# ScalarE's order of two steps in the expert loop of a hybrid transformer trunk

## The reference

```python
def swiglu(x, wg, wu, wd):
    return (jax.nn.silu(x @ wg) * (x @ wu)) @ wd

def moe_ffn(x, router_w, wg, wu, wd):          # D_FF_EXPERT = 1408, N_EXPERTS = 8, TOP_K = 2
    logits = (x @ router_w).astype(jnp.float32)
    top_val, top_idx = lax.top_k(logits, TOP_K)
    w = jax.nn.softmax(top_val, axis=-1)
    gate = jnp.sum(jax.nn.one_hot(top_idx, N_EXPERTS, dtype=jnp.float32) * w[..., None], axis=-2).astype(x.dtype)
    y = jnp.zeros_like(x)
    for e in range(N_EXPERTS):
        y = y + gate[..., e:e + 1] * swiglu(x, wg[e], wu[e], wd[e])
    return y
```

## Time and profile before

| | us |
|---|---|
| median of three timed runs | 1394.48 |
| lowest and highest of them | 1392.77, 1395.32 |
| the profiled execution | 1394.32 |
| its span, first to last instruction | 1392.5 |
| mean granted TensorE clock in it | 0.991 of full speed |

### The profile page before, as it was taken

How to read it: one execution, slowest core, us unless ns; L and a number is a source line. 1 busy time by engine, 2 the same in 40 slices (tenths; PEclk the granted TensorE clock), 3 DMA queues, 4 the chain that set the end, 5 groups by cost and what they waited for, 6 DMA issues and landing times.

```text
span 1392.5 us, 25141 instructions
## 1 busy us (share of the span) xinstructions
PE 1318.3 (95%) x10385; PEld 818.8 (59%) x10385; DVE 995.9 (72%) x1611; ACT 680.9 (49%) x1018; POOL 131.5 (9%) x113
## 2 busy tenths in 40 slices
PE   7999899999999999999999899989999999999992
PEld 4357444444444444444356444569979988978971
DVE  6986797685640456334986886678788888888886
ACT  6245675353210232112245764365576676676672
POOL 0010420410000000030001000501200000000003
PEclk9999999999999999999999999999999999999996
DMA  9330784334220343015220000158999999999975
GB/s 320 106 91 16 257 294 136 136 136 167 106 91 0 136 170 132 0 31 212 71 84 24 16 1 16 61 200 334 360 375 360 322 337 378 357 330 367 343 272 198
DMA packets 39999, 255.70 MB, mean 184 GB/s; under 512 B 5626, under 2 KB 6650, under 8 KB 25418
## 3 DMA queue, kind: packets, MB, share of 16 engines
q1 hardware_dynamic: 30490, 220.20, 42.7%
q0 software_dynamic: 8960, 33.26, 7.2%
q10 hardware_dynamic: 432, 0.59, 0.1%
HBM read 218.28 MB, written 33.65 MB: 181 GB/s over the span
## 4 chain that ended last, share of the span: by engine, by line
PE 75%; DVE 14%; ACT 6%; issue 2%; DMA 2%; SPq 0%; POOL 0%; ACTq 0%; DVEq 0%
PE bank L1117 19%; PE bank L1119 18%; PE bank L1118 18%; DVE arena L928 6%; ACT arena L785 5%; PE bank L1338 3%; PE bank L1384 2%; PE bank L1354 2%; DVE bank L2108 2%; DVE arena L2131 2%; PE bank L1245 1%; PE bank L1182 1%; PE bank L1244 1%; PE bank L1232 1%; ACT arena L1654 1%
## 5 line engine op out<-in xcount | busy, mean ns | idle before, releaser
L928 DVE SCALAR_TENSOR_TENSOR arena<-arena 128x3072 f16<-128x3072 f32 x86 | 288.8, 3358 | 57.1 <-ACT arena L785 56.4
L785 ACT ACTIVATE arena<-arena 128x3072 f16<-128x3072 f32 x86 | 237.0, 2756 | 0.1
L1117 PE MATMUL bank<-arena 128*128 128x144 bf16 (+3 forms) x894 | 219.4, 264 | 11.5 <-DVE arena L928 5.1
L1119 PE MATMUL bank<-arena 128*128 128x144 bf16 (+3 forms) x894 | 219.2, 264 | 0.0
L1118 PE MATMUL bank<-arena 128*128 128x144 f16 (+3 forms) x894 | 219.2, 264 | 0.0
L1117 PE MATMUL bank<-hh,wring_hi 128*128 128x512 bf16 x352 | 133.9, 381 | 0.0
L1119 PE MATMUL bank<-hh,wring_lo 128*128 128x512 bf16 x352 | 133.7, 380 | 0.0
L1118 PE MATMUL bank<-hl,wring_hi 128*128 128x512 f16 x352 | 133.7, 380 | 0.0
L1119 PE MATMUL bank<-hh,arena 128*128 128x512 bf16 x338 | 128.1, 379 | 0.0
L1118 PE MATMUL bank<-hl,arena 128*128 128x512 f16 x338 | 128.1, 379 | 0.0
L1117 PE MATMUL bank<-hh,arena 128*128 128x512 bf16 x338 | 128.1, 379 | 0.0
(11 more groups left out here) (336 smaller groups left out, 2669.8 us busy)
## 6 DMA issues: line engine op xcount, KB each, us to landing
arena<-in_ew SPq DMA_DIRECT2D x86, 1536.0 KB, 9.0
arena<-in_dw SPq DMA_DIRECT2D x22, 1536.0 KB, 6.7
wstage<-in_w_chunk SPq DMA_DIRECT2D x44, 512.0 KB, 3.6
expert_results<-iota POOLq DMA_DIRECT2D x9, 2048.0 KB
arena<-in_cmp_w SPq DMA_DIRECT2D x2, 2048.0 KB, 9.8
expert_slots<-iota POOLq DMA_DIRECT2D x5, 512.0 KB
expert_results<-wstage SPq DMA_DIRECT2D x5, 512.0 KB
arena<-in_w_tok SPq DMA_DIRECT2D x2, 1096.0 KB, 7.1
```

What stands on the lines that cost most here:

```text
L785: act.activation(ew_hi_[:, G % EP, :], ew[:, G % ES, :], ACT.Copy, scale=SW).then_inc(M["hi_ready"], 1)
L928: dve.scalar_tensor_tensor(out=ew_lo_[:, G % EP, :], in0=ew[:, G % ES, :], scalar=SW, in1=ew_hi_[:, G % EP, :], op0=ALU.mult, op1=ALU.subt ...
L1117: pe.matmul(out, w_hi, x_hi, start=first, stop=False)
L1119: return pe.matmul(out, w_lo, x_hi, start=False, stop=last)
```

## The change

ScalarE's order within a chunk is turned round from chunk 11 on (the second expert, n = 1). There `expert_hi(G + 2)` stands ahead of the wait for `up_mm` and the SiLU of chunk G. In chunks 0 to 10 the order stays. Its own waits (DMA of chunk G + 2, `down_stream(G - 2)`), its size and count stay as they are, and nothing is changed on any other engine.

```diff
@@ -65,6 +65,7 @@
 LEAD = 2
+FIRST_TURN = FE // P
 NEG = -1.0e30
@@ -842,11 +843,13 @@
                 first_hi(p)
             for G in range(NG):
                 n, f = divmod(G, FC)
+                if FIRST_TURN <= G < NG - LEAD:
+                    expert_hi(act, G + LEAD)
                 act.wait_ge(M["up_mm"], G + 1)
                 if G >= 2:
                     act.wait_ge(M["product"], FC + G - 1)
                 silu(G % 2, bank[G % 2], CAPS[n])
-                if G < NG - LEAD:
+                if G < FIRST_TURN:
                     expert_hi(act, G + LEAD)
                 if G == LEAD:
                     act.wait_ge(*ready("lg_sub"))
```

## The result

The changed kernel takes **1377.3 us** (median of 4 runs, 1375.79 to 1378.96) against 1393.91 us for the kernel before (4 runs, 1392.77 to 1395.32): 16.6 us less, a ratio of 0.9878 with a 95% interval of 0.9866 to 0.9890. In a second comparison it was 1376.8 against 1392.87, ratio 0.9883 (0.9868 to 0.9899).

What follows compares the result with a forecast made beforehand. The bound was a ring of matmuls, SiLU, upper half and lower half. TensorE's 17.5 us of idle time, less 2, 1, 1.2, 0.8 and 2.5 us, left a 10 us gain: 1384.3 us, range 1379.5 to 1393.

Steps and rivals of the forecast that it cites:

- the ring: Matmuls, SiLU, upper half, lower half, matmuls wait for each other in turn: 9.27 us per two chunks in expert 7.
- the place of the gain: TensorE's waits for VectorE's lower halves in the expert loop, to fall from 12.5 to 5 us or less.
- expert 2 unchanged: Expert 2 (width 168), where TensorE's busy time already fills the length, should keep its 56.8 us.
- the shape of the new waits: VectorE's waits for upper halves under 15 us, from 47.4; ScalarE waits for TensorE's down ahead of the upper half.
- the transfers' rate is no floor: Against a rival, 13%: about 357 GB/s is the average to be had in the experts, giving about 1392 us.
- The ceiling: All TensorE idle time in the waits for lower halves: 12.5 us in 31 waits plus 0.16 each, 17.5 us.
- The start of each expert: Previous expert's results wait for a down at f = 0; 0.7 us stays at experts 3, 5 and 7, 2 us.
- Waits that stay: First two waits of expert 1 (chunks 12 and 13), 1 us; steps to wide experts 2 and 4, 1.2 us.
- VectorE is the fullest: Last five chunks of expert 7: VectorE needs 4.14 us a chunk against TensorE's 3.99, costing 0.8 us.
- The loads: Weight loads landing in 9.8 us make upper halves wait, 4.28 us a chunk; with a border loss, 2.5 us.
- L + 7.3: Loop of four chunks: landing time L, then upper half 2.76, SiLU to product 0.3, product 0.8, lower half 3.4 us.
- the rate in experts 1 and 3: Sign of the forecast: the DMA rate in experts 1 and 3 should rise to 375 GB/s or more.

Runs made afterwards that it cites:

- short loads: Changed kernel, loading only the gate and up parts of each chunk (1024 of 1536 KB) from chunk 22 on: 1376.96 us.
- one chunk less of lead: Kernel before and changed kernel, each load issued one chunk later from chunk 22 on: 1413.08 us in the old order, 1421.94 in the changed order.
- the same kernel: Changed kernel with the turned order from chunk 0 on instead of chunk 11: 1381.9 us in its first run, 1382.18 in its second.
- the kernel turned only in the narrow experts: Changed kernel with the turned order only in experts 1, 3, 5 and 7 (widths 112 and 128): 1386.48 us.
- the one turned from 1: Changed kernel with the turned order from chunk 1 on, chunk 0 in the old order: 1376.75 us.
- the one with one copy: Changed kernel plus one useless 128 x 512 copy between upper half and SiLU from chunk 11 on: 1383.32 us.
- The kernel turned only in the wide experts: Changed kernel with the turned order only in experts 2, 4 and 6 (widths 168, 144, 144): 1388.0 us.

## Why the prediction was wrong

**Right:** the bound (the ring), the place of the gain (TensorE's waits for lower halves), its sign, expert 2 unchanged (56.3 of 56.8 us), the shape of the new waits, and that the transfers' rate is no floor: the Trainium skill's 358 GB/s of "DMA: Bandwidth & Descriptors", section "Where 436 GB/s comes from", was exceeded over whole experts, 374, 367 and 371 GB/s in 1, 3 and 6.

**Wrong: terms of the sum, each too low on the gain.** Without the transposes' 1.1 us, the sum as measured is 18.9 - 2.6 = 16.3 us, against 17.5 - 7.5 = 10.

- *The ceiling* of 17.5 us. "9.4 + 3.1 = 12.5 us in 31 waits" plus 0.16 each is right for these 31, but short gaps that the view does not list add 1.4: 18.9.
- *The start of each expert*, 2 us for experts 3, 5 and 7, was not there. The whole of these experts has gaps of 0.5, 0.0 and 0.2 us, and the 0.5 stands at the end of 3. The reckoning put TensorE and the halves at the same point when the expert begins. In the changed kernel a lower half ends 1.0 us before its matmuls in the median of chunks 11 to 87, and up to 2.4; in the kernel before it is 0.1 us in most chunks. This lead was left out, and it covers the start: 0.3 us and more are left in experts 3 and 5.
- *Waits that stay*, 2.2 us, were right: 0.8 at chunks 12 and 13, and 0.6 and 0.5 at the steps to experts 2 and 4.
- *"VectorE is the fullest"*, 0.8 us in expert 7, was 0.2. Two chunks took 7.95 us there, TensorE's own work, and not 8.3 to 8.6: VectorE, 4.07 a chunk, drew on its lead, which falls from 1.0 us at chunk 83 to 0.1 at 86 and 87.
- *The loads*, 2.5 us charged, cost about 0.4 (chunk 15; 0.6 in expert 4 in the second profile), and nothing measurable from chunk 22 on (short loads: 1376.96 against 1377.3). The form L + 7.3 is about right, as the kernels with one chunk less of lead show. The step that failed is the landing time put into it, 9.8 us, and what the result was set against. L rose only to 9.2 in the median, and (9.2 + 7.3) / 4 = 4.13 us is under TensorE's 4.2 and VectorE's 4.14. And experts 1 to 6 averaged 4.41 to 5.12 a chunk after the change, transposes and wide widths included, so that a late load mostly met slack.

The two large errors are the loads (2.1 of 6.3 us) and the starts of the experts (2.0), then the ceiling (1.4). One more sign of the forecast missed by little: the rate in experts 1 and 3 rose to 374 and 367 GB/s, not to 375 or more.

The range ended at 1379.5 because "some of the losses named are sure". They were estimates, and each leaned the same way; the ceiling did too. The full count of gaps in the kernel before would have put its lower end at 1394.3 - 18.9 = 1375.4.

## What to carry to other kernels

Where an engine in a ring waits for an event that its next, longer instruction does not need, put that instruction first, if its own operands are surely there. Check every place at which they are not (the first chunks, the first after a scatter): in the steady state a load late by 2.0 us was free and one late by 2.6 or 3.0 us cost 0.4 to 0.6; at the very first chunk one late by 1.8 us cost 5. To size such a gain, count start-to-start gaps of the bound engine, not its marked idle time, and do not deduct border losses from it without a reason why run-ahead can't cover them.

## What the runs showed of the hardware

- After TensorE had stood 4.95 us at 934 to 939 us, its clock was granted at 0.70 and 0.61 in two stretches of 5 us; the first run of the same kernel, on another chip, shows 0.77 and 0.55. Other waits in the loop, of up to 2.2 us (the kernel before with late loads, at 1053.8), had no such effect.
- Stretches at the lower clock also came outside the loop with TensorE busy all the time: at 740 to 750 us with 0.81 and 0.51, in the profiles of the kernel turned only in the narrow experts and of the one turned from 1, and at 745 to 750 with 0.66 in the one with one copy. Ten of the sixteen profiles, the kernel before among them, show 0.55 to 0.69 at 120 to 125 us. The kernel turned only in the wide experts shows 0.66 to 0.72 at 770, 910 and 925 us. By the start of the same matmul in a profile without the stretch, those looked at cost 1.0 to 3.3 us each. Nothing was changed there, and what brings them stays open. Timed runs of kernels that differ by less can't be told apart without looking at them.
- The chip loaded at 430 GB/s over a stretch of 4 us in the kernel before, at 374 over expert 1 of the changed kernel and at 386 over its expert 4 (1154.3 to 1205 us). Its loads of 1536 KB landed in 9.2 us in the median, in 10.1 in expert 1.
